# Mixer projections of chunks 3 to 10 in three passes, with their remainders on GpSimd

## What is computed

```
proj = h @ w_in[l]                      # 256 x 1024 by 1024 x 4352, plus 16 step-size columns
y_a = gelu(rg_gate) * rg_lru(causal_dwconv(rg_x), ...)
y_b = mamba2_group(z, xbc, dt_raw, ...)  # convolution, silu, chunked state-space scan, gated norm
y_c = sliding_window_attention(q, k, v, sinks)
h = layer_norm(ALPHA * h + concat(y_a, y_b, y_c) @ w_out[l])
h = layer_norm(ALPHA * h + peer_ffn(h))
```

```
r = sigmoid(...); i = sigmoid(...)
log_a = -8 * r * softplus(-lam)
a = exp(log_a)
u = sqrt(1 - a*a) * (i * x)             # written sqrt(-expm1(2*log_a))
h_t = a_t * h_(t-1) + u_t
```

## Time and profile before

| | us |
|---|---|
| median of 3 runs | 3117.61 (3115.69 to 3119.06) |
| the profiled execution | 3116.25 |
| its span in the profile | 3114.5 |
| TensorE busy | 2990.0 (96%) |
| VectorE busy | 2357.4 (76%) |
| ScalarE busy | 1531.1 (49%) |
| GpSimd busy | 295.4 (9%) |

### The profile page before, as it was taken

The page is one execution under the profiler, slowest core; times in us unless marked ns, Lnnn a source line. Parts: engine busy times, 40 slices in busy tenths (PEclk is TensorE's granted clock), DMA queues, the critical chain, the costliest instruction groups (busy, mean ns, idle before and its releaser), DMA issues.

```text
span 3114.5 us, 51411 instructions
## 1 busy us (share of the span) xinstructions
PE 2990.0 (96%) x16392; PEld 2511.5 (81%) x16392; DVE 2357.4 (76%) x5192; ACT 1531.1 (49%) x2678; POOL 295.4 (9%) x412
## 2 busy tenths in 40 slices
PE   7999999989989999999999999999999999999998
PEld 4888887869887879877888888778798778888887
DVE  5888888466656767997777777777679977777776
ACT  3222223245744655285555554446552855555544
POOL 0000000000000005191000000000051910000000
PEclk9999999999999999999999999999999999999999
DMA  6333332223222334314555555533344135555554
GB/s 272 117 118 110 118 133 99 95 72 136 82 95 99 119 127 158 136 42 146 186 187 186 186 187 199 178 109 109 135 150 135 41 135 189 189 189 189 188 189 135
DMA packets 74106, 440.83 MB, mean 142 GB/s; under 512 B 6976, under 2 KB 7360, under 8 KB 33152
## 3 DMA queue, kind: packets, MB, share of 16 engines
q1 hardware_dynamic: 71312, 420.23, 38.0%
q0 software_dynamic: 2528, 18.02, 1.6%
q10 hardware_dynamic: 144, 0.98, 0.1%
HBM read 438.16 MB, written 1.05 MB: 141 GB/s over the span
## 4 chain that ended last, share of the span: by engine, by line
PE 83%; DVE 9%; DVEq 2%; issue 2%; ACT 2%; ACTq 0%; DMA 0%; POOL 0%; SPq 0%
PE bank L474 17%; PE bank L476 17%; PE bank L475 17%; PE bank L2360 10%; PE bank L2362 5%; PE bank L2291 4%; DVE arena L2562 3%; PE bank L1531 2%; PE bank L890 1%; PE bank L879 1%; PE bank L1248 1%; PE bank L1266 1%; PE bank L561 1%; DVE arena L1583 1%; DVEq L2562 1%
## 5 line engine op out<-in xcount | busy, mean ns | idle before, releaser
L453 ACT ACTIVATE peer_r<-wring 128x512 fp32r<-128x512 f32 x1328 | 826.3, 631 | 807.4 <-PE bank L476 537.7
L458 DVE TENSOR_TENSOR peer_r<-wring,peer_r 128x512 fp32r<-128x512 f32 x1264 | 856.7, 691 | 389.1 <-ACT peer_r L453 385.8
L2360 PE MATMUL bank<-res_r,peer_r 128*128 128x512 f32 x1344 | 479.9, 397 | 3.4 <-DVE peer_r L458 3.4
L474 PE MATMUL bank<-h_r,peer_r 128*128 128x512 f32 (+1 forms) x1088 | 397.6, 365 | 23.5 <-DVE h_r L669 14.8
L474 PE MATMUL bank<-peer_r 128*128 128x512 f32 x1024 | 404.4, 395 | 2.8 <-DVE peer_r L2593 2.8
L476 PE MATMUL bank<-peer_r 128*128 128x512 f32 x1024 | 401.3, 392 | 0.0
L475 PE MATMUL bank<-peer_r 128*128 128x512 f32 x1024 | 399.5, 390 | 0.0
L476 PE MATMUL bank<-h_r,peer_r 128*128 128x512 f32 (+1 forms) x1088 | 385.3, 354 | 0.0
L2362 PE MATMUL bank<-res_r,peer_r 128*128 128x256 f32 x1344 | 376.9, 280 | 0.0
L475 PE MATMUL bank<-h_r,peer_r 128*128 128x512 f32 (+1 forms) x960 | 335.1, 349 | 0.0
L2360 PEld LDWEIGHTS bank<-res_r,peer_r 128*128 128x128 f32 x1344 | 252.5, 188 | 64.2 <-DVE peer_r L458 4.0
(11 more groups left out here) (395 smaller groups left out, 5016.4 us busy)
## 6 DMA issues: line engine op xcount, KB each, us to landing
wring<-in_w_peer SPq DMA_DIRECT2D x256, 1024.0 KB, 4.8
wring<-in_w_proj SPq DMA_DIRECT2D x34, 1024.0 KB, 4.8
wring<-in_w_hy SPq DMA_DIRECT2D x32, 1024.0 KB, 5.0
arena<-in_w_ada POOLq DMA_DIRECT2D x16, 1024.0 KB, 5.0
wring<-in_w_out SPq DMA_DIRECT2D x16, 1024.0 KB, 4.8
wring<-in_w_ada SPq DMA_DIRECT2D x8, 1024.0 KB, 11.3
wring<-in_w_hyout SPq DMA_DIRECT2D x8, 1024.0 KB, 4.8
wring<-in_w_q SPq DMA_DIRECT2D x8, 1024.0 KB, 4.8
```

What stands on the lines that cost most here:

```text
L453: act.activation(SPLIT[:, buf, 0, :], raw_quarter(name, i, j, q), ACT.Copy).then_inc(split_hi, 1)
L458: v.tensor_tensor(SPLIT[:, buf, 1, :], raw_quarter(name, i, j, q), SPLIT[:, buf, 0, :].bitcast(F32), ALU.subtract).then_inc(split_lo, 1)
L474: pe.matmul(out_ap, w_hi, x_hi, start=start, stop=False, **kw)
L2360: pe.matmul(two_parts(acc[:, :]), SPLIT[:, buf, 0, w], h_both[:, k, :, :], start=(k == 0), stop=False, skip_group_check=True)
```

## The change

- `SPLIT_FROM` is 3: chunks 3 to 16 go through `proj_split`, chunks 0 to 2 stay plain.
- GpSimd makes the low parts of all 14 of them (`proj_pool`, 56 a layer); VectorE's 24 are gone. VectorE waits for the last of them before it makes those of the output projection.
- ScalarE's high parts are interleaved by hand through `mixer_scalar`.
- The rows of `h` are split at the mixer's head, ahead of `decay_scalar` and `softplus_rows`, that is while TensorE makes the step-size product.
- 1 - a*a is taken as th * (1 + a*a): ScalarE squares a (RG[:, 3] into RG[:, 5]) at the end of `gates_scalar`, and VectorE has one product left. The add and the reciprocal are gone.
- Buffers of the window attention leave the region of `SPLIT`; the low rows go to the second half of `res`.

```diff
@@ buffers
-SPLIT_FROM = 11
+SPLIT_FROM = 3
-        MH_LO = view(arena_r("mh_lo", RG_AT, KT * T)[:, :], KT)
+        PT3 = c3.take(2, 3 * P)
+        VTK = c3.take(2, P)
+        ST = [c3.take(8, 8) for n in range(2)]
+        YQ = Carve(RG_AT).take(KT, T)
-        cw = Carve(BLOCKS * T)
+        cw = Carve()
-        YQ = tmp
+        MH_LO = h_hi
@@ remainders and rows
-        def proj_lo(v, l, j, quarters):
-            for q in quarters:
-                lo_quarter(v, f"proj{l}", 0, j, q, proj_unit(l, j, q), q, q == UNITS - 1)
+        def proj_pool(pool, l):
+            pool.wait_ge(split_lo, proj_unit(l, SPLIT_FROM, 0))
+            for j in range(SPLIT_FROM, 17):
+                for q in range(UNITS):
+                    lo_quarter(pool, f"proj{l}", 0, j, q, proj_unit(l, j, q), q, q == UNITS - 1)
+        ROWS_ORDER = (1, 3, 0, 2)
         def rows_scalar(act, l):
-            for k2 in range(4):
+            act.drain()
+            for n, k2 in enumerate(ROWS_ORDER):
+                if n >= 2:
+                    act.wait_ge(h_tok, 4 * l + n + 1)
@@ mixer_tensor: proj_chunk becomes proj_split for j = 3 to 10
@@ gates_scalar
+                if t == 2:
+                    proj_hi(act, l, 4, (0,))
-            act.drain().then_inc(a_ready, 1)
+            act.drain()
+            act.activation(RG[:, 5, :], RG[:, 3, :], ACT.Square).then_inc(a_ready, 1)
@@ mixer_scalar
+            rows_scalar(act, l)
             decay_scalar(act, l)
-            for j in range(3):
+            for j in range(2):
                 proj_out(act, l, j)
+            proj_hi(act, l, 3, range(4))
+            proj_out(act, l, 2)
             gates_scalar(act, l)
+            proj_hi(act, l, 4, (1, 2))
             proj_out(act, l, 3)
+            proj_hi(act, l, 4, (3,))
             values_scalar(act, l)
             root_scalar(act, l)
+            proj_hi(act, l, 5, range(3))
             proj_out(act, l, 4)
+            proj_hi(act, l, 5, (3,))
+            proj_hi(act, l, 6, (0,))
             exps_scalar(act, l, 0)
+            proj_hi(act, l, 6, (1, 2))
             for m0 in range(3):
                 proj_out(act, l, 5 + m0)
+                proj_hi(act, l, 6 + m0, (3,))
                 turned_scalar(act, l, m0)
+                proj_hi(act, l, 7 + m0, (0, 1))
                 silu_scalar(act, l, m0)
+                proj_hi(act, l, 7 + m0, (2,))
                 exps_scalar(act, l, m0 + 1)
             proj_out(act, l, 8)
-            rows_scalar(act, l)
+            proj_hi(act, l, 9, (3,))
             turned_scalar(act, l, 3)
+            proj_hi(act, l, 10, (0, 1))
             silu_scalar(act, l, 3)
+            proj_hi(act, l, 10, (2,))
             proj_out(act, l, 9)
+            proj_hi(act, l, 10, (3,))
...
-            act.wait_ge(sw_pv, 4 * l + 4)
-            proj_hi(act, l, 11, range(4))
+            proj_hi(act, l, 11, range(3))
             proj_out(act, l, 10)
             segment_scalar(act, l, 1)
+            proj_hi(act, l, 11, (3,))
@@ root_vector
-            v.tensor_scalar(u, th, 1.0, None, ALU.add)
-            v.drain()
-            v.reciprocal(u, u)
-            v.drain()
-            v.scalar_tensor_tensor(u, th, 2.0, u, ALU.mult, ALU.mult).then_inc(root_in, 1)
+            v.scalar_tensor_tensor(u, u, 1.0, th, ALU.add, ALU.mult).then_inc(root_in, 1)
@@ mixer_vector: rows_vector moves to the head, every proj_lo goes
+            rows_vector(v, l)
             softplus_rows(v, l)
...
+            v.wait_ge(split_lo, unit_of(f"out{l}", 0, 0))
@@ gpsimd, per layer
+                proj_pool(pool, l)
                 pre_pool(pool, l)
```

More of the change, by code:

```diff
@@ L258, in program @@
         TSD, TNM = stats[:, 28:30], stats[:, 30:32]
-        cw = Carve(BLOCKS * T)
+        cw = Carve()
         SM = [cw.take(2, 2 * T) for n in range(2)]
-        PT3 = cw.take(2, 3 * P)
-        VTK = cw.take(2, P)
-        ST = [cw.take(8, 8) for n in range(2)]
-        assert cw.at <= BLOCKS * T + 2 * UNITS * UNIT
+        assert cw.at <= KT * T
         G = arena[:, 0:BLOCKS * T].rearrange("p (j t) -> p j t", j=BLOCKS)
@@ L1553, in proj_hi @@
                 hi_quarter(act, f"proj{l}", 0, j, q, proj_unit(l, j, q), q)
-        def proj_lo(v, l, j, quarters):
-            for q in quarters:
-                lo_quarter(v, f"proj{l}", 0, j, q, proj_unit(l, j, q), q, q == UNITS - 1)
+        def proj_pool(pool, l):
[4 more added lines that the diff above has]
+        ROWS_ORDER = (1, 3, 0, 2)
         def rows_scalar(act, l):
-            for k2 in range(4):
+            act.drain()
+            for n, k2 in enumerate(ROWS_ORDER):
+                if n >= 2:
+                    act.wait_ge(h_tok, 4 * l + n + 1)
                 act.activation(two_tiles(MH_HI, k2), two_tiles(h, k2), ACT.Copy).then_inc(mh_hi, 1)
         def rows_vector(v, l):
-            for k2 in range(4):
-                v.wait_ge(mh_hi, 4 * l + k2 + 1)
+            for n, k2 in enumerate(ROWS_ORDER):
+                v.wait_ge(mh_hi, 4 * l + n + 1)
                 v.tensor_tensor(two_tiles(MH_LO, k2), two_tiles(h, k2), two_tiles(MH_HI, k2).bitcast(F32),
@@ L1782, in mixer_tensor @@
             rows_tensor(pe, l)
-            proj_chunk(pe, l, 3)
+            proj_split(pe, l, 3)
             values_tensor(pe, l)
-            proj_chunk(pe, l, 4)
+            proj_split(pe, l, 4)
             scores_tensor(pe, l, 0)
-            proj_chunk(pe, l, 5)
+            proj_split(pe, l, 5)
             scores_tensor(pe, l, 1)
@@ L1790, in mixer_tensor @@
             for m0 in range(2):
-                proj_chunk(pe, l, 6 + m0)
+                proj_split(pe, l, 6 + m0)
                 scores_tensor(pe, l, 2 + m0)
@@ L1794, in mixer_tensor @@
                 turned_tensor(pe, l, 1 + m0)
-            proj_chunk(pe, l, 8)
+            proj_split(pe, l, 8)
             mixed_tensor(pe, l, 2)
@@ L1799, in mixer_tensor @@
             front_tensor(pe, l, 0)
-            proj_chunk(pe, l, 9)
+            proj_split(pe, l, 9)
             mixed_tensor(pe, l, 3)
@@ L1804, in mixer_tensor @@
                 front_tensor(pe, l, t + 1)
-                (proj_split if t else proj_chunk)(pe, l, 10 + t)
+                proj_split(pe, l, 10 + t)
                 output_tensor(pe, l, t)
@@ L2155, in mixer_vector @@
             window_out(v, l, 2)
-            rows_vector(v, l)
             cb_vector(v, l, 0)
@@ L2164, in mixer_vector @@
             conv_vector(v, l, 5)
-            proj_lo(v, l, 11, range(4))
             sum_vector(v, l, 0)
@@ L2168, in mixer_vector @@
             inputs_vector(v, l, 2)
-            proj_lo(v, l, 12, range(3))
             sum_vector(v, l, 1)
             decayed_vector(v, l, 2)
-            proj_lo(v, l, 12, (3,))
             inputs_vector(v, l, 3)
-            proj_lo(v, l, 13, range(3))
             sum_vector(v, l, 2)
             decayed_vector(v, l, 3)
-            proj_lo(v, l, 13, (3,))
             cb_vector(v, l, 1)
             inputs_vector(v, l, 4)
-            proj_lo(v, l, 14, range(3))
             sum_vector(v, l, 3)
@@ L2183, in mixer_vector @@
             decayed_vector(v, l, 4)
-            proj_lo(v, l, 14, (3,))
             inputs_vector(v, l, 5)
             mix_vector(v, l, 0)
-            proj_lo(v, l, 15, range(3))
             sum_vector(v, l, 4)
             decayed_vector(v, l, 5)
-            proj_lo(v, l, 15, (3,))
             inputs_vector(v, l, 6)
@@ L2193, in mixer_vector @@
             v.drain().then_inc(mix_ready, 1)
-            proj_lo(v, l, 16, range(3))
             sum_vector(v, l, 5)
             decayed_vector(v, l, 6)
-            proj_lo(v, l, 16, (3,))
             inputs_vector(v, l, 7)
```

## The result

The changed kernel takes **3140.4 us** (3136.9 to 3142.4), the kernel before 3118.2 us beside it; the ratio is 1.0071 (95% interval 1.0054 to 1.0089). It is 22 us slower; 10 were forecast, with a range up to 3138. The profiled execution took 3141.8 us, with a span of 3139.7 against 3114.5, so the spans differ by 25.2 us.

What follows compares the result with a forecast made beforehand. It took VectorE, not TensorE, to set the pace up to the window loop's end. Per layer +11.8 - 6.4 - 0.5 = +4.9; twice 9.8, plus 0.5 once, +10.3 us: 3116.25 + 10.3 + 1.4 = 3128, range 3098 to 3138.

Steps and rivals of the forecast that it cites:

- case A: Rival: GpSimd doesn't hold convolutions or scans; rounds stay at 10.4 us, -18.8 us in all, 3099 us; chance 0.20.
- Rows split first: Mixer's head: copies and subtractions fit VectorE's 5.92 us wait in layer 0, cost nothing; 0.5 us once in layer 1.
- chunks of 5.8 us: TensorE: a chunk in three passes takes 5.8 us instead of 7.1 for a plain one.
- the wait for chunk 11's remainder: Chunks 9 to 11: TensorE's wait of 3.12 us for VectorE's remainders would be gone.
- Cases C and D: Rivals: TensorE starved by late low parts, 3156 us; first stages' chunks still 7.1 us, 3133 us; chance 0.06 together.
- Gates: Chunk 3's remainders hold the convolution: gate matmuls 3.8 us later, 1.8 hidden by ScalarE's table load, 2.0 left.
- Root stage: Reciprocal gone, remainders of chunks 4 and 5 hold VectorE: stage ends +0.7 to +4.1 us later, +1.5 taken.
- case B: Rival: GpSimd gets in only at VectorE's one-input instructions; -8.8 us in all, 3109 us; chance 0.18.
- Round 0: First round of the window-head loop: late eviction 0.75 us and four remainders in the convolution, +4.8 us.
- Rounds 1 and 2: Later rounds of the window-head loop: three remainders fall in each convolution, +2.75 us each.
- The sign given for line 1583: Profile after: convolution instructions with medians near 0.48 us but maxima over 1.4 us, some 20 a layer.
- Chunks 9 to 16: Behind the loop: -6.4 us for chunks 9 to 11, -0.5 from the wait at the end of chunks 12 to 16.

Runs made afterwards that it cites:

- experiment 1: Changed kernel with GpSimd's remainders cut from 512 to 8 columns in chunks 3 to 16, most low parts left out: 3111.8 us, ratio 0.9975.
- experiment 9: Experiment 1 with ScalarE's first three high parts of the next chunk moved behind the SiLU and exponentials in the window loop: 3103.8 us, ratio 0.9945.
- experiment 10: Changed kernel, all remainders computed, with ScalarE's high parts moved behind the SiLU and exponentials in the window loop: 3139.9 us, ratio 1.0065.
- experiment 2: Changed kernel with GpSimd's subtraction replaced by a memset of the same tile, which only writes; low parts left out: 3103.4 us in one execution.
- experiment 3: Changed kernel with the old root stage (add, reciprocal and product on VectorE, no Square on ScalarE): 3148.9 us, ratio 1.0093.
- experiments 5 to 8: Changed kernel with the split starting only at chunk 4, 9, 10 or 11: 3131.7, 3113.9, 3102.8 and 3113.1 us.

## Why the prediction was wrong, point by point

The direction was right, and so was the mechanism in outline: GpSimd's remainders hold VectorE, VectorE sets the pace from the root stage to the end of the loop, and the passes saved are not on the path there. The step that failed is the price of the holds: the prediction let GpSimd's remainders fall free of cost on TENSOR_SCALARs and, for the most part, between scans. The runs showed both held, nearly every time. The price of the holds as a whole, 29 us between the forecast and case A, was measured as 30 (experiment 1 against the change), but that agreement is partly luck. Between the traces of the two kernels the first maxima lie 9.1 and 7.4 us apart instead of 5.0, and what is behind the loop is 1.2 and 5.0 us longer in experiment 1, where nothing was forecast. The sum was 12 us too low in medians, 15 in spans. Its steps:

- **Rows split first; chunks of 5.8 us; the wait for chunk 11's remainder.** Right. In the trace after the four subtractions end at 937.4 and VectorE still has 1.5 us of its old wait for the step-size product left, 48 matmuls of a chunk take 5.7 us at full clock, and the wait of 3.1 us is gone. Cases C and D didn't happen: TensorE's waits for GpSimd's remainders are 1.7 us in layer 0.
- **Gates.** Forecast 3.8 us later at the start, 2.0 left at the sigmoids. They started 3.2 and 3.0 us later. In layer 1, at full clock, 2.3 us reached the sigmoids' end: right. In layer 0 it was 4.0 us, since TensorE ran at 0.69 behind its wait of 3.07 us: the gate products took 5.4 us instead of 3.7, and these 1.7 us are still there at the first maxima (49.8 against 48.1 us). This is the one place up to the loop where the clock's fall in the changed kernel stands on the path. The clock was named for another stretch, and not looked for where the change made a new wait.
- **Root stage: a term that failed.** +1.5 was taken, "nearer the lower end, since scans are issued without a pause between them"; +5.2 and +3.5 us were measured, against an upper bound of +4.1. The 1.7 us between the layers are the gates' clock, so the term itself is 2.0 too low. The four scans took 6.53 us instead of 2.44, so all four were held (+4.1), and the two products of 128x1024 took 2.29 and 2.22 instead of 1.2; the first of these two holds hides in a wait for ScalarE's root, of which 0.94 us is left. GpSimd and VectorE take turns here without a pause between the scans. The rows of the two copies, one right behind the other and both held, said so, and the prediction used them against case B but not here.
- **Round 0.** +4.8 forecast, +5.2 and +5.1 measured: the number is right, and in part by luck. Three instructions of the convolution took 4.41 us (1.61 before), +2.8. The other 2.4 us are three TENSOR_SCALARs, of 0.93, 1.39 and 1.10 us, which were thought to be free; the 0.75 us for the late eviction isn't in the round, 0.4 us of it lies ahead of it.
- **Rounds 1 and 2.** +2.75 each forecast, +3.9 and +3.7 measured. Two things were left out. A TENSOR_SCALAR was subtracted from each row of holds as if GpSimd could work beside it; it is itself held. This is the larger part of the error: of about 7.2 us by which VectorE's instructions are longer in these two rounds of layer 0, 6.2 are TENSOR_SCALARs, three of the convolution and four of two columns (up to 1.35 us instead of 0.23), and one SCALAR_TENSOR_TENSOR alone is held. The sign given for line 1583, some 20 held a layer, came out as 9. And even with no hold at all the two rounds grow by 3.5 us together (experiment 1), and by 1.9 us with the high parts behind the exponentials (experiment 9): ScalarE's queue, which the prediction priced at 0.75 us in round 0 and at nothing here, keeps either the exponentials or the eviction waiting (in layer 1 the two figures are 2.8 and 1.8 us). In the changed kernel this lies under the holds: moving the high parts there gave nothing in the time (experiment 10).
- **Chunks 9 to 16.** -6.9 forecast, -4.6 and -5.5 measured. Without holds and at full clock it was -6.4 (experiment 9, layer 0), and -2.5 in layer 1 with a half-clock stretch; with remainders that only write it was -6.4 and -6.6 (experiment 2). So the saving in passes was counted about rightly; what it lacks points to the held last convolutions (1.36 us for the TENSOR_SCALAR at 1040.57) and to the clock behind the loop's last wait of 5.9 us, which no run separated.
- **Case A's time.** 3099 forecast; 3111.8 (experiment 1), 3103.8 (experiment 9) and 3103.4 (experiment 2) measured. The last two are 5 us from it. Experiments 1 and 2 have the same order of work. Their traces differ by 13.7 us of span, 9.2 of it in the mixers, behind the loop and with another clock; but the trace of experiment 1 is its longest execution, so this tells of executions as much as of kernels.

The Trainium skill's rule (SBUF — State Buffer, "Who interferes with whom"), that a VectorE instruction with two SBUF inputs and a GpSimd instruction that reads exclude each other for the whole instruction, is what the scans and the convolution show (1.71 against 0.61 us, up to 1.57 against 0.48), and experiment 2 shows its other half: a GpSimd instruction that only writes left them at 0.67 and 0.48. The same section has the term that I left out: it lists tensor_scalar among the instructions that can take the shared pair of ports in a two-port mode, and then GpSimd is shut out or shuts them out. The trace agrees (0.88 us in the median against 0.41, and 0.61 beside a GpSimd that only writes). A row of the kernel before could have told it: the TENSOR_SCALAR of 128x1024 takes 0.69 us, while the two-input product of the same size takes 1.22, so it moves nearly two elements in the time of one. And the copies in rows 9, which the prediction used as its evidence, have one input and are both held.

What the range missed: its upper end took in the scans and some holds more, but not the one-input instruction, nor ScalarE's queue, nor the clock behind a new wait. With every scan held and a TENSOR_SCALAR counted like its neighbours, the prediction's own rows give +4.1 in the root stage and about +3.2 in each of the rounds, 3.5 us a layer more: 3135; with the 1.7 us of the gates' clock in layer 0, 3137.

## What to carry to other kernels

Before work is moved to an idle GpSimd, look at what VectorE does in the very microseconds in which it will run, and price each GpSimd instruction that meets work of a kind that is held, here 1.0 to 1.1 us for a GpSimd instruction of 1.29, whether or not there is a gap. Find the kinds in a trace of your own: here two-input instructions in on-chip memory and the TENSOR_SCALAR were held, while TENSOR_REDUCE, the reciprocal and instructions on accumulation banks were not. Where VectorE sets the pace, moving four remainders costs more than the shorter chunk can give; where TensorE does, they cost little: here the border lay between chunks 9 and 10, where one chunk more makes the two mixers 6 us longer. A fall of TensorE's clock costs only where TensorE is last, so fill its waits only there, and only after a trace has shown that nothing else is. And before two kernels a few microseconds apart are ranked, look whether their traces differ where the kernels do.

## What the runs showed that I had not expected

- A TENSOR_SCALAR with one tensor input in on-chip memory is held by a GpSimd subtraction as much as a two-input instruction is: 128x256 in 1.39 us instead of 0.41, 128x2 in 1.10 instead of 0.23. Beside the same subtractions a TENSOR_REDUCE stays at 0.69 us, a reciprocal of 128x1024 at 6.55 us (experiment 3), and a TENSOR_SCALAR from an accumulation bank at 0.34 us. A GpSimd instruction of 0.53 us that only writes holds it as well (0.61), and leaves SCALAR_TENSOR_TENSOR (0.489 at most) and TENSOR_TENSOR_SCAN (0.694) alone.
- TENSOR_TENSOR_SCAN of 128x256 is held each time when GpSimd has work queued: 1.71 us instead of 0.61, eight of eight.
- GpSimd is stretched too: four remainders took 6.95 us beside the scans, 1.74 us each, where one alone takes 1.29 (at 973.92).
- The granted clock was 0.53 to 0.69 in the mean of the stretches behind TensorE's waits of 3.07, 2.80, 6.39 and 5.87 us in layer 0's mixer, and with the waits filled it stayed at 1.00 there, yet the rounds became at most 0.4 us shorter. Behind the same wait ahead of the gates in layer 1, 3.05 us, it was 1.00 without any filling.
- The part of the program that no experiment touches took between 2686.0 and 2696.6 us in the traces, a spread of the size of most differences in the table of experiments 5 to 8.
